# Ten instead of six tile pairs of the upward stage by seven products, eight of them in couples, with x kept in memory meanwhile

## What is computed

```python
def conv_ffn(h, w_up, conv_w, w_down):          # w_up: 1024 x 5632
    gu = causal_dwconv(h @ w_up, conv_w)        # three taps along the tokens
    g, u = jnp.split(gu, 2, axis=-1)
    return (jax.nn.silu(g) * u) @ w_down        # w_down: 2816 x 1024

x = x + y @ w_out[i]
x = x + conv_ffn(rmsnorm(x, norm_ffn_gain[i]), ffn_w_up[i], ffn_conv_w[i], ffn_w_down[i])
```

## Time and profile before

| | |
|---|---|
| median of three runs | 1214.38 us |
| the profiled execution's own time | 1214.4 us |
| its span, first to last instruction | 1212.6 us |
| PE busy | 1199.7 us (99%) |
| PEld, DVE, ACT, POOL busy | 994.6, 737.8, 639.0, 725.1 us |
| granted clock of PE | 0.999 |
| DMA engines' mean busy share | 32.2% on the main queue |

### The profile page before, as it was taken

The page is one execution under the profiler, slowest core; times in us unless marked ns, Lnnn a source line. Parts: engine busy times, 40 slices in busy tenths (PEclk is TensorE's granted clock), DMA queues, the critical chain, the costliest instruction groups (busy, mean ns, idle before and its releaser), DMA issues.

```text
span 1212.6 us, 19024 instructions
## 1 busy us (share of the span) xinstructions
PE 1199.7 (99%) x6883; PEld 994.6 (82%) x6883; DVE 737.8 (61%) x1322; ACT 639.0 (53%) x1235; POOL 725.1 (60%) x558
## 2 busy tenths in 40 slices
PE   9999999999999999999999999999999999999997
PEld 7977777777878899987897777878898988898886
DVE  6655427757646777645597555446777765966224
ACT  6365535676644444455644666556556644333543
POOL 6773232353259776856384557548676775886842
PEclk9999999999999999999999999999999999999999
DMA  7332222222223333354142123323243343334332
GB/s 248 103 98 75 62 62 62 53 67 74 70 62 101 95 98 99 102 185 117 50 117 62 44 71 96 103 72 96 71 121 88 106 121 84 91 96 118 109 88 70
DMA packets 62437, 112.27 MB, mean 93 GB/s; under 512 B 6856, under 2 KB 11464, under 8 KB 62344
## 3 DMA queue, kind: packets, MB, share of 16 engines
q1 hardware_dynamic: 62200, 111.06, 32.2%
q10 hardware_dynamic: 144, 0.00, 0.0%
HBM read 108.87 MB, written 2.16 MB: 92 GB/s over the span
## 4 chain that ended last, share of the span: by engine, by line
PE 94%; DVE 3%; ACT 1%; issue 1%; DMA 1%; SPq 0%; POOL 0%; DVEq 0%; ACTq 0%; POOLq 0%
PE pb L1165 21%; PE pb L1166 21%; PE pb L1168 21%; PE pb L1227 5%; PE pb L1229 5%; PE pb L1228 5%; PE pb L1383 2%; PE pb L1236 2%; PE pb L1359 2%; PE pb L1326 1%; PE pb L1297 1%; PE pb L1299 1%; PE pb L1298 1%; PE pb L1280 1%; PE pb L1278 1%
## 5 line engine op out<-in xcount | busy, mean ns | idle before, releaser
L2861 POOL TENSOR_TENSOR wlo<-raw,whi 128x512 fp32r<-128x512 f32 (+3 forms) x378 | 510.7, 1369 | 324.1 <-ACT whi L1592 320.1
L1165 PE MATMUL pb<-HH,whi 128*128 128x512 f32 x760 | 307.6, 405 | 0.0
L1166 PE MATMUL pb<-HL,whi 128*128 128x512 f32 x760 | 300.5, 395 | 0.0
L1168 PE MATMUL pb<-HH,wlo 128*128 128x512 f32 x760 | 299.7, 394 | 0.0
L1592 ACT ACTIVATE whi<-raw 128x512 fp32r<-128x512 f32 (+3 forms) x377 | 222.9, 614 | 107.2 <-PE pb L1168 55.8
L1165 PEld LDWEIGHTS pb<-HH,whi 128*128 128x128 f32 x760 | 143.2, 188 | 37.5 <-issue 4.6
L1166 PEld LDWEIGHTS pb<-HL,whi 128*128 128x128 f32 x760 | 143.0, 188 | 33.6 <-issue 2.9
L1168 PEld LDWEIGHTS pb<-HH,wlo 128*128 128x128 f32 x760 | 142.9, 188 | 33.3
L1728 ACT ACTIVATE P<-P,stat 128x256 f32<-128x256 f32 (+3 forms) x96 | 50.6, 527 | 78.3 <-DVE stat L2418 56.6
L2095 DVE SCALAR_TENSOR_TENSOR cv<-pb,vecs,cv 128x511 f32<-128x511 f32 x88 | 65.6, 745 | 5.4 <-ACT cv L1992 3.9
L2083 DVE TENSOR_TENSOR pb<-pb,rff 128x512 f32<-128x512 f32 x44 | 30.0, 695 | 40.7 <-PE pb L1168 34.0
(11 more groups left out here) (489 smaller groups left out, 2795.1 us busy)
## 6 DMA issues: line engine op xcount, KB each, us to landing
raw<-in_wall SPq DMA_DIRECT2D x368, 256.0 KB, 2.7
raw<-in_wall SPq DMA_DIRECT2D x8, 260.0 KB, 3.0
X<-in_xT SPq DMA_DIRECT2D x8, 256.0 KB, 5.3
X<-in_xT SPq DMA_DIRECT2D x2, 1024.0 KB, 8.7
outT<-PP SPq DMA_DIRECT2D x8, 256.0 KB, 2.5
raw<-in_wall SPq DMA_DIRECT2D x10, 192.0 KB, 2.4
raw<-in_wall SPq DMA_DIRECT2D x9, 128.0 KB, 2.3
cst<-in_cst SPq DMA_DIRECT2D x1, 832.0 KB, 7.6
```

The lines of the kernel that those rows point to most:

```text
L1165: pe.do.matmul(b, hi, xh[k], start=start, stop=False, skip_group_check=tile[0] == "down")
L1166: pe.do.matmul(b, hi, xl[k], start=False, stop=False, skip_group_check=tile[0] == "down")
L1168: m = pe.do.matmul(b, lo, xh[k], start=False, stop=stop, skip_group_check=tile[0] == "down")
L2861: g.do.tensor_tensor(lo, x, hi.bitcast(F32), ALU.subtract).then_inc(*up(name, point))
```

## The change

- `UPS` is (6, 7, 9, 10, 12, 13, 15, 16, 18, 20) instead of (6, 8, 10, 12, 14, 16). Four times two pairs stand side by side, called a couple here, with A the first and B the second.
- All splits of a pair are asked for five units ahead, S2's too; those of B therefore fall into A, and the last two of B stand behind A's S4.
- `scaled`, `taps`, `swish` of tile j - 1 stand behind product A11 instead of S2, with the product of j - 2 if j - 1 is plain; `taps` of the up half behind S1; `product` of j - 1 behind S3.
- The planner marks as pending also the up half, cd, sx and sz, and gives a bank back (`let_go`) at the step of its last reader, with a new time; the choice goes by that time.
- The token sums of kp 2 and 3 go where x lies, those of kp 1 to tile 20's place. x is written to memory (two transfers of 1 MB, SP) behind tile 0 and read back in the second downward tile; `product8` at S2 waits for it, the token sums of kp 2 and 3 for the writing. The products of tiles 16 to 19 wait no longer for the last pair.

```diff
--- before.py
+++ after.py
@@ -32,7 +32,7 @@
 TURN = [(d, n) for d in range(8) for n in "cab"]
 PAIRS = [tuple((d, BRANCH[n]) for d, n in TURN[i:i + 2]) for i in range(10, 24, 2)]
 NGATE = len(PAIRS)
-UPS = (6, 8, 10, 12, 14, 16)
+UPS = (6, 7, 9, 10, 12, 13, 15, 16, 18, 20)
 NUP = NGATE + len(UPS)
 DOWN = [("tile", d) for d in range(4)] + [(x, n) for q in range(4) for x, n in (("pair", q), ("tile", 4 + q))]
 DOWN_BANK = {"tile": (0, 1, 2, 3, 6, 1, 4, 5), "pair": ((4, 5), (7, 0), (2, 3), (7, 0))}
@@ -203,7 +203,21 @@
     def add(self, *step):
         self.steps.append(step)
         if step[0] == "product":
-            self.pending.discard(("ffn", 0, step[1]))
+            self.let_go(("ffn", 0, step[1]))
+        elif step[0] == "taps" and step[1]:
+            self.let_go(("ffn", 1, step[2]))
+        elif step[0] == "product7" and step[2] == "S3" and NGATE <= step[1] < NUP:
+            self.let_go(("cd", UPS[step[1] - NGATE]))
+        elif step[0] == "split" and self.units[step[1]][1] and NGATE <= self.units[step[1]][1][0] < NUP:
+            p, x = self.units[step[1]][1]
+            if x in ("S3", "S4"):
+                self.let_go(("sx" if x == "S3" else "sz", p))
+
+    def let_go(self, tile):
+        self.pending.discard(tile)
+        if self.holder.get(self.bank[tile]) == tile:
+            self.clock += 1
+            self.held[self.bank[tile]] = self.clock
 
     def take(self, ring, tile):
         banks = {"main": (0, 1, 2, 3), "first2": (0, 1), "last2": (2, 3), "ups": (0, 1, 2), "any": tuple(range(8)), "S": (), "Y": (7,), "m3": (0, 1, 2), "x5": (3, 4, 5, 6, 7),
@@ -222,7 +236,7 @@
         bank = min((b for b in range(8) if b not in self.kept and self.holder.get(b) not in self.pending),
                    key=lambda b: self.held.get(b, -1))
         self.hold(bank, tile)
-        if tile[:2] == ("ffn", 0):
+        if tile[0] in ("ffn", "cd", "sx", "sz"):
             self.pending.add(tile)
         if keep:
             self.kept[bank] = tile
@@ -335,19 +349,21 @@
             if p < NGATE:
                 self.hold(3 + i, ("acc", p, x))
         for x in FACTORS:
-            if not (NGATE <= p < NUP and x == "S2"):
-                self.split_to(self.unit_of[p, x] + LOOK)
+            self.split_to(self.unit_of[p, x] + LOOK)
             self.add("product7", p, x)
-            if NGATE <= p < NUP and x == "S2":
-                j = UPS[p - NGATE] - 1
-                self.split_to(self.unit_of[p, x] + NS)
+            if not NGATE <= p < NUP:
+                continue
+            j = UPS[p - NGATE] - 1
+            if x == "A11":
+                if j not in UPS:
+                    self.add("product", j - 1)
                 self.add("scaled", 1, j)
                 self.add("taps", 0, j)
                 self.add("swish", j)
-                self.add("product", j - 1)
-            if x == "S3" and NGATE <= p < NUP:
-                self.add("taps", 1, UPS[p - NGATE] - 1)
-                self.add("product", UPS[p - NGATE] - 1)
+            elif x == "S1":
+                self.add("taps", 1, j)
+            elif x == "S3":
+                self.add("product", j)
 
     def turns(self, units):
 
@@ -675,6 +691,8 @@
                     add("t_sums", 3, sums_of[j])
                 elif j in sums_of:
                     add("t_parts", 3, sums_of[j])
+                if half and j == 0:
+                    add("x_away")
         add("taps", 1, NPAIR - 1)
         add("product", NPAIR - 1)
         for kp in range(4):
@@ -687,6 +705,8 @@
         parts_at = {(1, 6): 0, (2, 0): 1, (2, 8): 2, (3, 2): 3}
 
         def between(d, i):
+            if (d, i) == (1, 2):
+                add("x_back")
             if (d, i) in parts_at:
                 add("t_parts", 1, parts_at[d, i])
             if d == 7:
@@ -703,6 +723,7 @@
                 if n == 5:
                     add("p_parts")
                 continue
+            self.pending.clear()
             for i, t in enumerate(("ab", "cd")):
                 self.hold(DOWN_BANK[x][n][i], ("dn", n, t))
             if n == 3:
@@ -1061,7 +1082,8 @@
         FH = [a3(f"fh{j}", T, F32R)[:, :] for j in range(NPAIR)]
         FL = [a3(f"fl{j}", T, F32R)[:, :] for j in range(NPAIR)]
         ffn_work = a3.p
-        sums_places = [(ffn_work, ffn_work + 8 * T)] + [(place[f"fh{j}"], place[f"fl{j}"]) for j in (16, 18, 20)]
+        sums_places = [(ffn_work, ffn_work + 8 * T), (place["fh20"], place["fl20"]),
+                       (arena + 16 * T, arena), (arena + 24 * T, arena + 8 * T)]
         THU, TLU = ([tensor_at(f"tu{n}{kp}", [P, 2 * T], F32R, sums_places[kp][x]) [:, :] for kp in range(4)]
                     for x, n in enumerate("hl"))
         TSU = [tensor_at(f"tus{kp}", [P, 2 * T], F32, sums_places[kp][1])[:, :] for kp in range(4)]
@@ -1080,6 +1102,7 @@
         acc4, rs4 = a4("acc4", T)[:, :], a4("rs4", T)[:, :]
 
         scratch = nc.dram_tensor("decays", (2, 2, 8, T), F32, kind="Internal").ap()
+        x_kept = nc.dram_tensor("x_kept", (P, KD * T), F32, kind="Internal").ap()
         pb = [ctx.enter_context(nc.psum_tensor(f"pb{i}", [P, T], F32)) for i in range(8)]
 
         def ps(*tile):
@@ -1110,7 +1133,8 @@
 
         names = ["landed_gain", "landed_vec", "landed_cst", "landed_masks", "landed_sums", "landed_decay", "landed_rgw", "landed_p",
                  *(f"landed_raw{i}" for i in range(NR)), *(f"landed_x{i}" for i in range(KD)),
-                 *(f"landed_xr{i}" for i in range(2)),
+                 *(f"landed_xr{i}" for i in range(2)), *(f"landed_away{i}" for i in range(2)),
+                 *(f"landed_back{i}" for i in range(2)),
                  *(f"stored{i}" for i in range(2)),
                  "proj", "product", "small", "scored", "turned", "valued", "hgrn", "summed",
                  "whi", "xhi", "a_out", "a_exp", "a_turn", "a_norm", "a_gate", "a_small", "a_hg",
@@ -1608,6 +1632,11 @@
                     a.wait_ge(*at("full", ("wout", 7)))
                     a.wait_ge(*at("x_ffn", 7))
                     a.wait_ge(*at("mix_lo", 7))
+                    if kp > 1:
+                        a.wait_ge(*at("h3_lo", 7))
+                        a.wait_ge(*at("sum3"))
+                        for i in range(2):
+                            a.wait_ge(*at("x_away", i))
                     a.do.activation(TSU[kp][:, 0:T], xk[kp], ACT.Copy, scale=gain).then_inc(*up("a_t7"))
                     a.do.activation(ps("ts", kp, 0)[:, H:T], xk[kp][:, H:T], ACT.Copy, scale=gain).then_inc(*up("a_t7"))
                     a.do.activation(ps("ts", kp, 1), xk[kp + 4], ACT.Copy, scale=vecs("ffn_norm", kp + 4)).then_inc(
@@ -1999,7 +2028,7 @@
 
             def product(j):
                 a.wait_ge(*at("product", j))
-                if j > 15:
+                if j > 19:
                     a.wait_ge(*at("product7", NUP - 1, "S3"))
                 a.do.activation(FH[j], cv[(3 * j + 2) % 6], ACT.Copy).then_inc(*up("xhi", ("f_hi", j)))
 
@@ -2295,6 +2324,7 @@
                     v.do.tensor_tensor(dst, one, two, ALU.add).then_inc(*up("v_c7", *points))
 
                 if x == "S2":
+                    v.wait_ge(*at("x_back", q // 2))
                     v.wait_ge(*at("product7", p, "S2"))
                     v.wait_ge(*last("v_c7"))
                     v.do.tensor_copy(U7, ps("dn", q, "ab")[:, left]).then_inc(*up("v_c7"))
@@ -3032,6 +3062,19 @@
                 s.wait_ge(*at("full", ("wo", 7)))
                 s.do.dma_start(RGW[:, :], rgw).then_inc(*landing("landed_rgw", ("rgw",)))
 
+            def x_away():
+                for i in range(2):
+                    s.wait_ge(*at("x_ffn", 4 * i + 3))
+                    s.do.dma_start(x_kept[:, 4 * T * i:4 * T * i + 4 * T], X[:, 4 * T * i:4 * T * i + 4 * T]).then_inc(
+                        *landing(f"landed_away{i}", ("x_away", i)))
+
+            def x_back():
+                s.wait_ge(*at("product7", NUP - 1, "S3"))
+                for i in range(2):
+                    s.wait_ge(*at("x_away", i))
+                    s.do.dma_start(X[:, 4 * T * i:4 * T * i + 4 * T], x_kept[:, 4 * T * i:4 * T * i + 4 * T]).then_inc(
+                        *landing(f"landed_back{i}", ("x_back", i)))
+
             def p_in():
                 s.wait_ge(*at("full", ("ffn", 1, NPAIR - 1)))
                 s.wait_ge(*at("f_lo", NPAIR - 1))
@@ -3052,7 +3095,7 @@
                     s.wait_ge(*at("stored", i))
 
             follow({"split": lambda u: load_to(plan.last_load[u] + NR), "begin": begin, "decay": decay, "masks": masks,
-                    "x_again": x_again, "begin2": begin2, "p_in": p_in, "half_out": half_out, "end": end})
+                    "x_again": x_again, "begin2": begin2, "x_away": x_away, "x_back": x_back, "p_in": p_in, "half_out": half_out, "end": end})
 
         programs = (sync, scalar, vector, pool, tensor)
         for program in programs:
```

## The result

The changed kernel takes 1218.49 us (median of seven runs, 1217.42 to 1219.24), the kernel before beside it 1214.43 us: a ratio of 1.0031, 95% interval 1.0021 to 1.0042. It is slower by 4.1 us, although PE has less to do.

What follows compares the result with a forecast made beforehand. PE was taken to bound the kernel: 1214.4 - 5.4 (matmuls) - 1.1 (banks) + 10.45 (couples) = 1218.4 us. Own range 1216.4 to 1221 us (0.64); 8 in 10: 1209.5 to 1222.

Steps and rivals of the forecast that it cites:

- The matmuls: PE, upward stage: four pairs more at 1.35 us each, 5.4 us off; pair 9.81 us, plain tile 11.16 us.
- The couples: Upward stage: DVE's work in A delays B's splits; 2.5 us for the first couple, 2.65 each after, 10.45 us added.
- The ledger of DVE's queue: DVE's operations in a couple added up in program order from trace prices, counted from A's first matmul, against PE's deadlines.
- The three waits: PE in B: before S2 (DVE), S1 (POOL), A12 (u on DVE); cumulative 1.05, 1.75, 2.5 us.
- nearly all of a couple: Profile sign: DVE busy for nearly all the time of a couple, put at 22.1 to 22.3 us.
- the third station: B's A12 waits for u on DVE: u ends at 19.3, due at 16.8; cumulative wait 2.5 us.
- Banks given back: Upward pairs, product A22: the new planner's bank order removes the wait for an earlier up half's taps; 1.1 us off.
- x to memory: Two 1 MB writes and reads on SP's queue: 0 cost, some 25 us of cover for weights; upper bound 5 us.
- Only the first wait: Rival, 0.17: a couple costs only 1.05 us, 1212.1 us in all; with the second wait too, 1214.9.
- slow transfers: Rival, 0.05: the forecast's mechanism plus weights late behind a write of x; 1222 to 1226 us.
- banks not given back in time: Rival: the 1.1 us stay and a couple also waits for a bank at B.A22; 1219.5 to 1221 us.
- couples at PE's pace: Rival, 0.14: the ledger overstates and B finds everything ready, so couples lose nothing; 1207.9 us.

Runs made afterwards that it cites:

- e7_singles_banks_kept: The changed kernel with eight single pairs (tiles 6, 8, ... 20), none side by side, and the old bank rule; 1209.8 us, ratio 0.9952.
- e9: Against e4_reordered: behind a couple or pair, taps of the up half moved right behind the plain tile's first taps; 1208.33 us, ratio 0.9943.
- e11: Against e9: the taps of tile 4's up half stand early too, ahead of the first couple; 1207.77 us, ratio 0.9942.
- e4_reordered: Changed kernel, couples reordered: in A up-half taps before the copy of u, product behind B's splits; in B tanh behind u's copy; 1211.18 us, ratio 0.9972.
- e6: Changed kernel with one of two taps left out of the up half ahead of each couple; 1215.76 us, ratio 1.0013.
- e2_six: Changed kernel with the six old pair tiles (6, 8, ... 16), keeping x to memory, new bank rule and moved front steps; 1217.96 us.
- e3: Changed kernel; in a couple's first pair the product of the tile before stands behind the splits of B.S1 and B.S3; 1219.57 us, ratio 1.0039.
- e5: Changed kernel with the front steps put back where they stood before, couples kept; 1234.44 us, ratio 1.0166.
- e8: Against e4_reordered: in B the copy of u stands ahead of the first taps and of the next split; 1214.97 us, ratio 1.0007.

## Why the prediction was right, and where it was not

**The matmuls** came out as counted: 9.82 and 9.74 us for the pairs at 18 and 20, 11.16 to 11.18 us for the plain tiles.

**The couples.** The ledger of DVE's queue held to 0.05 us at every step that I had named: u of A at 6.31 (6.28 predicted), the sums at 8.21 (8.18), the product at 11.06 (11.04), the low part of B.S2 at 13.67 (13.65), u of B at 18.92 (18.87). The three waits stand where they were said to be. Of the share of DVE the forecast said "nearly all of a couple"; it is 18.77 of 22.34 us, with the two idle stretches of 1.54 us that the ledger itself had at 1.48. Shown, not only argued: one operation less in the queue moved all three stations by its length, and waits taken away at the first two stations came back at the third.

**The size** was a little off. A couple was put at 2.5 us first and 2.65 us later, and is 2.7 in all four. The lateness at the third station was right: PE resumes at 19.40 us, due at 9.82 + 7.03 = 16.85, so 2.55 us late. On top comes the restart, which the sum did not have: the first matmul is 0.22 instead of 0.117 us ahead of the second, and the 24 matmuls of A12 and S4 take 2.94 instead of 2.79 us. Since the first couple is longer by this, the second one finds DVE at 888.36 - 887.70 = 0.66, not 0.85; so it loses no more than the first.

**Banks given back** was the wrong name on the right time, 1.1 us forecast and 1.2 to 1.3 measured. It is gone, but with single pairs it is gone under the old rule as well. For a pair behind a plain tile A22's bank had been the up half of the pair before under both rules; what changed is that its taps are done sooner, since the moved steps bring DVE forward. Taps of the up half ahead of the fifth pair, on DVE, in the kernel before and in e7_singles_banks_kept:

```profile
939.44 1.52 DVE L2095 SCALAR_TENSOR_TENSOR cv<-pb,vecs,cv 128x511 f32<-128x511 f32 x2
```

```profile
937.34 1.52 DVE L2121 SCALAR_TENSOR_TENSOR cv<-pb,vecs,cv 128x511 f32<-128x511 f32 x2
```

Before, they end at 940.96, 1.8 us after the pair's first matmul (939.20), and A22 goes on at 941.01. In e7 they end at 938.86, 0.8 us ahead of the pair (939.66). The step that failed is the one that read the new bank rule as the cause. What the rule does in the couples alone was not tried.

**x to memory** at 0 was right: 6.3 us to land, no wait, and 1212.43 us with the six old tiles. The reason given, the lead of the weights, fits the trace: the slowest loads around the two transfers landed 1.1 and 3.4 us later than the slowest at the same places in the kernel before, against some 25 us of cover by the count of units.

**The rivals.** *Only the first wait* fell with the second and third, *slow transfers* and *banks not given back in time* with the list of waits, in which nothing stands for weights or before B.A22. The rival of couples at PE's pace was wrong for this order of steps, and right as a possibility: e9 and e11 are that rival, with the same DVE operations in another order, at 1208.3 and 1207.8 us against 1207.9 computed for it. By occupancy, the Trainium skill's measure (Perfetto Trace Analysis, Identifying the Most-Contended Engine), DVE is busy for 84% of the first couple in the changed kernel, for 92% in e4_reordered (18.86 of 20.50 us) and for 91% in e11_first_couple (17.75 of 19.59): PE waited longest where the share was lowest. The share says that there is work to fill, and the queue read in order says what this kernel does.

The sum hit 1218.4 for 1218.49 partly by chance: the term of the couples misses by 0.3 us (10.8 for 10.45), that of the banks by 0.1 to 0.2 us the other way, and the runs scatter by 1.8 us.

## What to carry to other kernels

Before work is taken from the engine that bounds a kernel, write the queue of the next engine, in program order, from start-to-start times in the trace, against the deadlines of the first; a mean load of 90% says nothing about a stretch in which two dense pieces touch. Where PE waits at several places for the same in-order queue, the waits are one lateness: take time out ahead of the first or shorten the whole round, best by moving a ready operation into an idle stretch, and look at the next round before believing in a gain at one deadline. After any change of a planner's rule look at the places with a written table beside it.

## What the runs showed of the hardware

A wait of PE cost about 0.25 us more than the idle time that the profile shows: the first couple's three idle stretches are 1.04 + 0.44 + 0.49 = 1.97 us, and it lost 2.72. In e6 they are 1.20 us for 1.94 lost. Some 0.16 us of the 0.25 is how the profile counts: the idle time begins where the last matmul's record ends, 0.28 us after its start, while in a full queue the next one starts after 0.117. The rest is the restart, the first matmul being 0.20 to 0.22 us ahead of the second.

After some waits, and not after others, PE's granted clock fell to the lower level for 3.4 us: after 3.79 us idle in e2_six, after 2.42 and 2.43 us in e3's second and fourth couple but not after 2.47 us in its first; in e5 at three of four idle stretches of 3.61 us, the last time for 6.8 us. Before each of these long waits, with a fall or without, PE had run for more than 25 us without a wait and at the higher level. Idle stretches up to 1.04 us, twelve in the changed kernel, and four of 1.14 to 1.19 us in e8 were followed by no fall.
